# A second-half row of inverse deviations through DRAM instead of TensorE, in a fused conformer convolution layer

## The chip, the cores and the metric

One Trainium2 chip, one core. The metric is the device time of the kernel in microseconds (us); the kernel before took 353.53 us, the median of three runs (353.43 to 353.73). The engines go by short names: PE is TensorE, DVE is VectorE, ACT is ScalarE, POOL is GpSimd, SP is SyncE, which issues most DMAs. Each engine works through its own list in order; semaphores order the engines against each other.

## The reference

With one layer, the reference is an RMS norm, a gated depthwise convolution with a layer norm, and an output projection, added to x. Tokens T = 1024, channels D = 1024, 31 taps, all in float32:

```
hn = x * rsqrt(mean(x*x)) * norm_g
a, b, gate = split(hn @ w_in, 3)
u = causal_conv(a * sigmoid(b), conv_w) + conv_b         # per channel
uf = (u - mean(u)) * rsqrt(var(u) + eps) * ln_g + ln_b   # over channels
y = x + (silu(uf) * silu(gate)) @ w_out
```

## The kernel before

Activations lie with channels on the partitions: 8 channel tiles (k) of 128, and two halves (h) of 512 tokens. To keep float32 precision every matmul operand is split into a high part (x_hi, w_hi, wb_hi; made by ACT) and a remainder (x_lo, w_lo, wb_lo; made by DVE or POOL), and each product is three matmuls of 128 x 512.

The input projection is 24 units of 128 output channels (m = 0 to 23: pairs b and a, then 8 gates), each for both halves, 8 steps of three matmuls (`project`). The convolution runs behind it on DVE, ACT and POOL. The layer norm needs sums over channels, so over partitions: ACT and DVE split the convolution's words in two planes, a DMA transposes them, ACT and DVE join them (`join_half`, L932 and L1207), DVE takes statistics with tokens on the partitions (`take_stats`, `moments`), and POOL makes the inverse deviations (`inverse_deviation`, L1427), 128 x 4 numbers for each half. To use them with channels on the partitions again, a row of 512 tokens has to stand on all 128 partitions. For that PE multiplies a broadcast column by the identity (`spread_mean`, `spread_rstd`), four columns for each half and each of the two quantities, put between the steps of units 22 and 23 (`MEAN_SPREAD_AT`, `RSTD_SPREAD_AT`: unit, half, step). The result is in PSUM (`norm_spread`); ACT copies the deviations to SBUF as well (`copy_rstd`), because POOL's share of the first half's scalings (`POOL_SCALES`) reads them there.

Then, tile by tile: DVE subtracts the mean (`centre`), DVE or POOL multiplies by the deviation (`scale`), ACT applies SiLU with ln_g and ln_b into one of two PSUM banks (`act_norm`, which waits for the bank that the gate two tiles earlier frees), DVE multiplies by the gate (`gate`), and ACT and DVE split the result (`split_v`).

The output projection is done as seven block products (b = 0 to 6, `out_product`) of sums of blocks, a Strassen-like scheme; each has 4 pieces q of 128 tokens with 12 matmuls each. PE waits at a block's start for its operands (`wait_operands`: the x_lo by DVE, the wb_lo by DVE or POOL), and at each piece for a free bank, which an addition on DVE (`post`) frees. The sums of operands are `sum_v` on DVE and `w_out_op` on POOL, where `W_PAUSES` lets POOL wait for DVE's splits. All orders are written out by hand: the lists at the top, and each engine's own program in its block.

The lines that the rows name: L654 units' matmuls, L711 and L721 the spreads of means and deviations, L730 output products; L1211 DVE's half of the join, L936 ACT's; L1199 statistics, L1217 moments, L1223 `centre`, L1244 and L1470 `scale` on DVE and POOL, L1252 `gate`, L1259 `split_v`, L1279 `sum_v`, L1291 `post`; L947 `act_norm`, L851 reads a unit, L961 ACT's `split_v`; L1434 deviations, L1478 weight remainders of the output, L1462 those of the input; L930 the split of words; L671 and L798 the first units and x splits; L1158 the convolution's input.

Of the kernel before, what the change touches and what calls it, by code (L numbers as in the profile page):

```python
# [5 lines left out]
F32 = mybir.dt.float32  # L6
# [5 lines left out]
P = 128  # L12
# [28 lines left out]
MEAN_SPREAD_AT = {(22, 1, 2): 0, (22, 1, 6): 1}  # L41
RSTD_SPREAD_AT = {(22, 1, 4): 0, (23, 0, 0): 1}
# [32 lines left out]
SPREAD_AT = {1: (0, 4), 0: (3, 0, 1)}  # L75
CK = 4
# [23 lines left out]
def gated_conv_layer(nc, x, x_t, w_first, w_in, w_out, per_channel, identity, out):  # L100
# [31 lines left out]
    with ctx:  # L132
# [52 lines left out]

        acc = ctx.enter_context(nc.psum_tensor("acc", [P, 4, HALF], F32))
# [54 lines left out]
        rstd_ready = sem("rstd_ready")  # L241
        mean_spread = sem("mean_spread")
# [63 lines left out]
        def norm_spread(h, what):  # L306

            return acc[:, 2 * h + what, :]

# [201 lines left out]
        def _(sp):  # L511
# [79 lines left out]
            sp.wait_ge(wlo_ready, NU - 3)  # L591
            load_w_out("a", 0, 0, 1)
            sp.wait_ge(steps_done, len(STEPS))
            sp.wait_ge(sums_done, len(SUMS))
            load_w_out("b", 1, 0, 0)
            load_w_out("a", 1, 0, 1)
            for i in range(2):
                sp.wait_ge(wb_done, W_OP["lo", 0, i])
                load_w_out("b", i, 1, 0)
# [186 lines left out]
        def _(act):  # L786
# [151 lines left out]
            def copy_rstd(h):  # L938

                act.wait_ge(rstd_spread, h + 1)  # L940
                nc.scalar.activation(rstd_row(h), norm_spread(h, 1), ACT.Copy).then_inc(rstd_copied, 1)
# [67 lines left out]
            for m in range(2, NU):  # L1009
# [6 lines left out]
                for i, h in enumerate(half_order(m)):  # L1016
# [13 lines left out]
                    if (m, h) == (NU - 2, 1):  # L1030
                        copy_rstd(0)
                        for k in range(2):
                            act_norm(k, 0)
                    if (m, h) == (NU - 1, 0):
                        for k in range(2, 4):
                            act_norm(k, 0)
                        copy_rstd(1)
                        for k in range(4, 6):
                            act_norm(k, 0)
                    if (m, h) == (NU - 1, 1):  # L1040
                        for k in range(CK):
                            split_v(0, k)
                        act_norm(6, 0)
                        act_norm(7, 0)
# [36 lines left out]
        def _(dve):  # L1081
# [287 lines left out]
            for k in range(CK):  # L1369
                scale(k, 1)  # L1370
            for k in range(CK, KC):
                centre(k, 1)
            for k in range(CK):
                split_v(0, k)
# [8 lines left out]
            for k in range(2, KC):  # L1383
                gate(k, 1)
            posts(1, (0,))
            for k in range(CK):
                sum_v(2, k)
            posts(1, (1,))
            for k in range(CK):
                split_v(2, k)  # L1390
# [25 lines left out]
            posts(4, (2,))  # L1416
# [4 lines left out]
            posts(4, (3,))  # L1421
# [4 lines left out]
        def _(pool):  # L1426
# [27 lines left out]
            def finish_w_lo(m):  # L1454

                pool.wait_ge(whi_ready, m - 1)
                if m == 2:
                    nc.gpsimd.tensor_tensor(w_lo[:, 2, 0:KC // 2, :].rearrange("p k n -> p (k n)"), raw[:, 0, 0:HALF],
                                            w_hi[:, 2, 0:KC // 2, :].rearrange("p k n -> p (k n)").bitcast(F32),
                                            ALU.subtract).then_inc(w2lo_half_ready, 1)  # L1460
                ks = slice(KC // 2 if m == 2 else 0, KC)
                nc.gpsimd.tensor_tensor(w_lo[:, m % 3, ks, :].rearrange("p k n -> p (k n)"), raw[:, m % 2, ks.start * P:],  # L1462
                                        w_hi[:, m % 3, ks, :].rearrange("p k n -> p (k n)").bitcast(F32),
                                        ALU.subtract).then_inc(wlo_ready, 1)
# [86 lines left out]
            for h in range(NH):  # L1551
                inverse_deviation(h)
                w_out_op(*W_OPS[h])
# [56 lines left out]
```

## Time and profile before

| | |
|---|---|
| median of 3 runs | 353.53 us (353.43 to 353.73) |
| the profiled execution | 355.37 us, span from first to last instruction 353.6 us |
| PE busy | 348.6 us, 99%, 1564 matmuls |
| DVE busy | 323.1 us, 91% |
| ACT busy | 229.7 us, 65% |
| POOL busy | 258.9 us, 73% |
| granted TensorE clock | 1.0 of full speed in all 40 slices |
| chain that ended last | PE 92%, DMA 3%, SP's queue 3%, ACT 1% |

The busy shares say which engine has no idle time. The chain of waits is followed back from the last instruction, at each step to what released it, and so tells whose time the end depends on. The timelines give single instructions: start, duration, engine, line, what is written from what, and in brackets the idle time before it and what ended that.

### The profile page before, as it was taken

The page shows a single profiled execution, that of the slowest core. Times are in us where ns is not written, and L with a number is a line of the kernel's source. Part 1 is how long each engine was busy: PE and PEld are TensorE (multiplying, and loading weights), DVE is VectorE, ACT ScalarE, POOL GpSimd, SP SyncE. Part 2 cuts the span into 40 slices and gives each one's busy share as a digit, 9 for nine tenths or more (in the row PEclk, how much of TensorE's full clock was granted, in tenths as well). Part 3 has the DMA queues.
Part 4 walks back from the last instruction along what each step waited for, and adds up shares of the span by engine and source line. Part 5 has one row for each costly group of instructions (what it writes and reads, how often), then busy time and mean ns, then how long its engine had stood idle before and what let it go on. Part 6 is the DMA issues. An engine that isn't in the chain of part 4 may idle for free.

```text
span 353.6 us, 4764 instructions
## 1 busy us (share of the span) xinstructions
PE 348.6 (99%) x1564; PEld 289.3 (82%) x1564; DVE 323.1 (91%) x523; ACT 229.7 (65%) x330; POOL 258.9 (73%) x189
## 2 busy tenths in 40 slices
PE   8989999999999999999999999999999999999996
PEld 7868888888888888888888888888888888888886
DVE  4759799999999999999999999999699999999962
ACT  5979784667947780998669777984576773443400
POOL 0027999999999999689999999897596550406150
PEclk9999999999999999999999999999999999999999
DMA  7995111111410141404110410441743399074142
GB/s 253 411 412 196 61 61 53 66 62 59 119 48 14 62 119 59 119 0 121 59 44 19 119 59 3 119 119 38 235 145 119 93 371 346 25 239 142 68 177 90
DMA packets 30520, 43.51 MB, mean 123 GB/s; under 512 B 18336, under 2 KB 18848, under 8 KB 30496
## 3 DMA queue, kind: packets, MB, share of 16 engines
q1 hardware_dynamic: 30352, 43.21, 36.5%
q8 instruction: 12, 0.20, 0.2%
q14 instruction: 12, 0.10, 0.1%
q10 hardware_dynamic: 144, 0.00, 0.0%
HBM read 34.82 MB, written 4.19 MB: 110 GB/s over the span
## 4 chain that ended last, share of the span: by engine, by line
PE 92%; DMA 3%; SPq 3%; ACT 1%; issue 0%; DVE 0%
PE mm L654 68%; PE acc L730 12%; PE mm L730 9%; DMA sgate<-x 3%; SPq L518 2%; PE mm L671 2%; SPq L542 1%; PE acc L711 1%; PE acc L721 1%; SPq L514 0%; ACT sgate L792 0%; PE acc L648 0%; ACT x_hi L798 0%; PE acc L642 0%; SPq L548 0%
## 5 line engine op out<-in xcount | busy, mean ns | idle before, releaser
L654 PE MATMUL mm<-x_hi,w_hi 128*128 128x512 f32 x352 | 137.4, 390 | 0.0
L654 PE MATMUL mm<-x_hi,w_lo 128*128 128x512 f32 x352 | 137.0, 389 | 0.0
L654 PE MATMUL mm<-x_lo,w_hi 128*128 128x512 f32 x352 | 137.0, 389 | 0.0
L1191 DVE SCALAR_TENSOR_TENSOR acc<-u,chan,acc 128x512 f32<-128x512 f32 x157 | 110.8, 751 | 0.1
L1518 POOL TENSOR_TENSOR pconv<-pconv,prod 128x512 f32<-128x512 f32 x60 | 77.0, 1304 | 1.3 <-ACT prod L885 1.3
L654 PEld LDWEIGHTS mm<-x_hi,w_lo 128*128 128x128 f32 x352 | 66.1, 188 | 13.8
L654 PEld LDWEIGHTS mm<-x_hi,w_hi 128*128 128x128 f32 x352 | 66.1, 188 | 13.6
L654 PEld LDWEIGHTS mm<-x_lo,w_hi 128*128 128x128 f32 x352 | 66.1, 188 | 13.4
L1191 DVE SCALAR_TENSOR_TENSOR acc<-u,w_sum,acc 128x512 f32<-128x512 f32 x90 | 67.6, 752 | 2.1 <-ACT acc L867 2.0
L885 ACT ACTIVATE prod<-u,chan 128x512 f32<-128x512 f32 x69 | 47.9, 715 | 19.4 <-POOL pconv L1518 18.1
L1462 POOL TENSOR_TENSOR w_lo<-raw,w_hi 128x1024 fp32r<-128x1024 f32 (+1 forms) x21 | 49.6, 2362 | 7.6 <-ACT w_hi L834 7.6
L1518 POOL TENSOR_TENSOR pool_before<-pool_before,prod 128x512 f32<-128x512 f32 x37 | 48.1, 1301 | 1.1
L885 ACT ACTIVATE prod<-u,w_sum 128x512 f32<-128x512 f32 x30 | 21.4, 715 | 7.7 <-POOL pool_before L1518 7.4
L961 ACT ACTIVATE x_hi<-sgate 128x512 fp32r<-128x512 f32 x28 | 15.9, 624 | 15.7 <-DVE sgate L1279 15.7
L730 PE MATMUL acc<-wb_hi,x_hi 128*128 128x512 f32 (+1 forms) x68 | 25.7, 378 | 0.0
L730 PE MATMUL acc<-wb_hi,x_lo 128*128 128x512 f32 (+1 forms) x68 | 25.6, 377 | 0.0
L730 PE MATMUL acc<-wb_lo,x_hi 128*128 128x512 f32 (+1 forms) x68 | 25.6, 377 | 0.0
L834 ACT ACTIVATE w_hi<-raw 128x1024 fp32r<-128x1024 f32 x22 | 23.1, 1048 | 1.7 <-PE mm L654 1.7
L1478 POOL TENSOR_TENSOR wb_lo<-raw,wb_hi 128x1024 fp32r<-128x1024 f32 x5 | 12.0, 2399 | 14.3 <-DVE x_lo L1259 14.3
L911 ACT ACTIVATE sgate<-nat 128x1024 uint16<-128x1024 uint16 x14 | 14.0, 1049 | 11.5 <-POOL nat L1509 8.9
L924 ACT ACTIVATE rows<-sgate 128x1024 uint16<-128x1024 uint16 x14 | 18.3, 1372 | 3.6 <-DMA sgate<-sgate 2.3
L1451 POOL TENSOR_TENSOR x_lo<-nat,x_hi 128x512 fp32r<-128x512 f32 x16 | 20.2, 1304 | 0.0
(114 smaller groups left out, 520.8 us busy)
## 6 DMA issues: line engine op xcount, KB each, us to landing
raw<-w_in SPq DMA_DIRECT2D x22, 512.0 KB, 3.3
nat<-x_t SPq DMA_DIRECT2D x16, 256.0 KB, 6.0
sgate<-x SPq DMA_DIRECT2D x8, 512.0 KB, 11.6
raw<-w_out SPq DMA_DIRECT2D x8, 512.0 KB, 3.3
nat<-x SPq DMA_DIRECT2D x8, 512.0 KB, 7.7
y<-nat SPq DMA_DIRECT2D x15, 256.0 KB, 2.1
raw_late<-w_out SPq DMA_DIRECT2D x4, 512.0 KB, 4.2
sig<-w_out SPq DMA_DIRECT2D x4, 512.0 KB, 4.5
```

Source lines behind the costliest of these rows:

```text
L654: ins = nc.tensor.matmul(bank(("unit", m, h)), w[:, m % 3, k, :], xx[:, k, half(h)], start=(k == 0 and i == 0), stop=(k == KC - 1 and i == 2))
L730: ins = nc.tensor.matmul(product_bank(b, q), v[:, k0 + k, rows], w[:, k, piece_columns(b, q)], start=(k == 0 and i == 0 and continued(b, q ...
L834: nc.scalar.activation(w_hi[:, m % 3, :, :].rearrange("p k n -> p (k n)"), raw[:, m % 2, :], ACT.Copy).then_inc(whi_ready, 1)
L885: nc.scalar.activation(dst, chain_in(j, chain, k), ACT.Identity, scale=tap(j, chain, k), bias=bias(j, chain) if k == 0 else 0.0).then_inc( ...
L911: nc.scalar.activation(planes()[:, i * T:(i + 1) * T].rearrange("p (h s q) -> p h s q", h=NH, s=2), words(nat[:, j, :])[:, :, i].rearrange ...
L924: nc.scalar.activation(words_of_rows(side)[:, :, :, i], crossed()[:, NT * i:NT * (i + 1), :], ACT.Copy).then_inc(rows_joined, 1)
L961: nc.scalar.activation(v_pair(b, k)[0], v_raw(b, k), ACT.Copy).then_inc(vhi_ready, 1)
L1191: ins = nc.vector.scalar_tensor_tensor(dst, chain_in(j, chain, k), tap(j, chain, k), chain_bank(j, chain), ALU.mult, ALU.add)
L1451: nc.gpsimd.tensor_tensor(x_lo[:, k, half(h)], nat[:, k, half(h)], x_hi[:, k, half(h)].bitcast(F32), ALU.subtract).then_inc(xlo_pool, 1)
L1462: nc.gpsimd.tensor_tensor(w_lo[:, m % 3, ks, :].rearrange("p k n -> p (k n)"), raw[:, m % 2, ks.start * P:], w_hi[:, m % 3, ks, :].rearran ...
L1478: ins = nc.gpsimd.tensor_tensor(lo, source, hi.bitcast(F32), ALU.subtract)
L1518: ins = nc.gpsimd.tensor_tensor(pool_sum(chain), summand, prod[:, SLOTTED.index((j, chain, k)) % 4, :], ALU.add)
```

## The change

 - The second half's deviations are no longer spread by PE. SP stores the 128 x 4 numbers to a DRAM tensor and loads them back to all partitions as one row of 512 in the order token, tile; ACT copies the row to the PSUM bank that the spread used to fill, with the two orders swapped (a read with a step of four elements). This copy stands behind the activations of tiles 4 and 5, where the copy before stood ahead of them.
 - POOL makes both halves' deviations ahead of the first output weights' remainders; it did one, a remainder, the other, a remainder.
 - POOL's last remainder of the input weights waits for DVE's first copy of the join. SP loads one output weight ahead of that remainder's end.
 - PE spreads the means two steps sooner, the first half's deviations one step sooner, and the first half's root means (`SPREAD_AT`, at the start of the kernel) one step later.
 - On DVE, block 0's splits go ahead of four centrings, the first two additions of block 1 go ahead of two gates and two `sum_v`, and block 4's third additions go behind the operands of block 6.

```diff
--- before.py
+++ after.py
@@ -38,8 +38,8 @@
 ROWS_AT = {(7, 0): 0, (10, 0): 2, (12, 0): 1, (13, 1): 3, (16, 1): 5, (18, 1): 6, (20, 0): 4}
 CROSS_AFTER = {10: 0, 13: 2, 15: 1, 16: 3, 19: 5, 21: 6, 23: 4}
 STATS_AT = {10: [0], 14: [1], 19: [2]}
-MEAN_SPREAD_AT = {(22, 1, 2): 0, (22, 1, 6): 1}
-RSTD_SPREAD_AT = {(22, 1, 4): 0, (23, 0, 0): 1}
+MEAN_SPREAD_AT = {(22, 1, 0): 0, (22, 1, 4): 1}
+RSTD_SPREAD_AT = {(22, 1, 3): 0}
 POOL_SCALES = {0: (1, 3, 5, 7), 1: ()}
 
 
@@ -72,7 +72,7 @@
 ROW_ORDER = (4, 5, 6, 7, 0, 1, 2, 3)
 ROWS_BEFORE = {1: (4,), 2: (5,), 3: (6,), 4: (7,)}
 DIAGS_BEFORE = {4: (4, 5), 5: (6, 7)}
-SPREAD_AT = {1: (0, 4), 0: (3, 0, 1)}
+SPREAD_AT = {1: (0, 4), 0: (3, 0, 2)}
 CK = 4
 V_SOURCE = ((0, 0), (4, 0), (0, 0), (4, 1), (4, 1), (0, 1), (4, 0))
 V_SLOT = ((0, 0), (4, 0), (0, 1), (4, 1), (0, 0), (4, 0), (0, 1))
@@ -182,6 +182,8 @@
                 spare = sb("spare", [P, 2, KC * P])
             wb[slot] = [sb(f"wb_{part}{slot}", [P, CK, HALF], F32R) for part in ("hi", "lo")]
         raw_late = sb("raw_late", [P, KC * P])
+
+        rstd_dram = nc.dram_tensor("rstd_of_tokens", [P * TPH], F32, kind="Internal").ap()
 
         acc = ctx.enter_context(nc.psum_tensor("acc", [P, 4, HALF], F32))
         mm = ctx.enter_context(nc.psum_tensor("mm", [P, 4, HALF], F32))
@@ -239,6 +241,8 @@
         mv_ready = sem("mv_ready")
         veps_ready = sem("veps_ready")
         rstd_ready = sem("rstd_ready")
+        rstd_stored = sem("rstd_stored")
+        rstd_row_in = sem("rstd_row_in")
         mean_spread = sem("mean_spread")
         rstd_spread = sem("rstd_spread")
         rstd_copied = sem("rstd_copied")
@@ -306,6 +310,14 @@
         def norm_spread(h, what):
 
             return acc[:, 2 * h + what, :]
+
+        def by_token(row):
+
+            return row.rearrange("p (q t) -> p t q", t=TPH)
+
+        def by_tile(row):
+
+            return row.rearrange("p (t q) -> p t q", t=TPH)
 
         def rstd_row(h):
 
@@ -588,12 +600,16 @@
             load_w_out("b", 0, 0, 0)
             for h in range(NH):
                 cross_half(h)
-            sp.wait_ge(wlo_ready, NU - 3)
-            load_w_out("a", 0, 0, 1)
             sp.wait_ge(steps_done, len(STEPS))
             sp.wait_ge(sums_done, len(SUMS))
             load_w_out("b", 1, 0, 0)
+            sp.wait_ge(wlo_ready, NU - 3)
+            load_w_out("a", 0, 0, 1)
             load_w_out("a", 1, 0, 1)
+            sp.wait_ge(rstd_ready, NH)
+            sp.dma_start(rstd_dram.rearrange("(p t) -> p t", t=TPH), rstd[:, TPH:NT]).then_inc(rstd_stored, 16)
+            sp.wait_ge(rstd_stored, 16)
+            sp.dma_start(rstd_row(1), rstd_dram.partition_broadcast(P)).then_inc(rstd_row_in, 16)
             for i in range(2):
                 sp.wait_ge(wb_done, W_OP["lo", 0, i])
                 load_w_out("b", i, 1, 0)
@@ -935,10 +951,15 @@
                 act.wait_ge(stats_ready, NT * (KC // 2 - 1))
                 nc.scalar.activation(half_rows(h, 0), half_crossed(h, 0), ACT.Copy).then_inc(rows_joined, 1)
 
-            def copy_rstd(h):
-
-                act.wait_ge(rstd_spread, h + 1)
-                nc.scalar.activation(rstd_row(h), norm_spread(h, 1), ACT.Copy).then_inc(rstd_copied, 1)
+            def copy_rstd_row():
+
+                act.wait_ge(rstd_row_in, 16)
+                nc.scalar.activation(by_tile(norm_spread(1, 1)), by_token(rstd_row(1)), ACT.Copy).then_inc(rstd_copied, 1)
+
+            def copy_rstd():
+
+                act.wait_ge(rstd_spread, 1)
+                nc.scalar.activation(rstd_row(0), norm_spread(0, 1), ACT.Copy).then_inc(rstd_copied, 1)
 
             def act_norm(k, h):
 
@@ -1028,15 +1049,15 @@
                         act.wait_ge(sums_done, len(SUMS))
                         split_w_out(0, 0)
                     if (m, h) == (NU - 2, 1):
-                        copy_rstd(0)
+                        copy_rstd()
                         for k in range(2):
                             act_norm(k, 0)
                     if (m, h) == (NU - 1, 0):
                         for k in range(2, 4):
                             act_norm(k, 0)
-                        copy_rstd(1)
                         for k in range(4, 6):
                             act_norm(k, 0)
+                        copy_rstd_row()
                     if (m, h) == (NU - 1, 1):
                         for k in range(CK):
                             split_v(0, k)
@@ -1368,10 +1389,10 @@
             gate(3, 0)
             for k in range(CK):
                 scale(k, 1)
+            for k in range(CK):
+                split_v(0, k)
             for k in range(CK, KC):
                 centre(k, 1)
-            for k in range(CK):
-                split_v(0, k)
             for k in range(CK):
                 gate(CK + k, 0)
             for k in range(CK, KC):
@@ -1380,12 +1401,16 @@
             gate(1, 1)
             for k in range(CK):
                 split_v(1, k)
-            for k in range(2, KC):
+            for k in range(2, 6):
                 gate(k, 1)
             posts(1, (0,))
-            for k in range(CK):
+            for k in range(6, KC):
+                gate(k, 1)
+            for k in range(2):
                 sum_v(2, k)
             posts(1, (1,))
+            for k in range(2, CK):
+                sum_v(2, k)
             for k in range(CK):
                 split_v(2, k)
             for i in range(2):
@@ -1413,12 +1438,11 @@
                 split_v(5, k)
             posts(4, (1,))
             finish_wb_lo(5, 1)
-            posts(4, (2,))
             for k in range(CK):
                 sum_v(6, k)
             for k in range(CK):
                 split_v(6, k)
-            posts(4, (3,))
+            posts(4, (2, 3))
             for b in range(5, 7):
                 posts(b)
 
@@ -1454,6 +1478,8 @@
             def finish_w_lo(m):
 
                 pool.wait_ge(whi_ready, m - 1)
+                if m == NU - 1:
+                    pool.wait_ge(rows_by_vector, 1)
                 if m == 2:
                     nc.gpsimd.tensor_tensor(w_lo[:, 2, 0:KC // 2, :].rearrange("p k n -> p (k n)"), raw[:, 0, 0:HALF],
                                             w_hi[:, 2, 0:KC // 2, :].rearrange("p k n -> p (k n)").bitcast(F32),
@@ -1550,7 +1576,8 @@
             assert (due, summed) == (NU, KC)
             for h in range(NH):
                 inverse_deviation(h)
-                w_out_op(*W_OPS[h])
+            for op in W_OPS[0:2]:
+                w_out_op(*op)
             for k in POOL_SCALES[0]:
                 scale(k, 0)
             w_out_op(*W_OPS[2])
```

## Rows read from the trace of the kernel before

**Rows 1.** The page's busy engines: us, share of the span, instructions.
```profile
PE 348.6 (99%) x1564; PEld 289.3 (82%) x1564; DVE 323.1 (91%) x523; ACT 229.7 (65%) x330; POOL 258.9 (73%) x189
```

**Rows 2.** PE's waits: who waited for whom, us in total, times, longest.
```profile
PE mm L671 <- ACT x_hi L798: 1.1, 1, 1.1
```

**Rows 3.** The chain that ended last, in order: start, us, what.
```profile
255.74 0.89 PE acc L711 x8
...
262.58 0.89 PE acc L721 x8
```

**Rows 4.** Timeline of PE, output products: start, us, engine, line, operation.
```profile
274.20 0.47 PE L730 MATMUL acc<-wb_hi,x_hi 128*128 128x512 f32 x1
...
301.53 0.39 PE L730 MATMUL acc<-wb_hi,x_hi 128*128 128x512 f32 x1
...
328.73 0.39 PE L730 MATMUL mm<-wb_hi,x_hi 128*128 128x512 f32 x1
...
340.97 0.39 PE L730 MATMUL mm<-wb_hi,x_hi 128*128 128x512 f32 x1
```

**Rows 5.** Timeline of DVE, from the join to block 0's splits.
```profile
250.28 1.49 DVE L1211 COPY rows<-sgate 128x512 uint16<-128x512 uint16 x1 [2.64 <-DMA sgate<-sgate]
251.81 1.41 DVE L1199 BATCH_NORM_STATS2 stats<-rows 128x6 f32<-128x256 f32 x4
...
253.79 0.40 DVE L1211 COPY rows<-sgate 128x512 uint16<-128x512 uint16 x1
...
255.67 0.63 DVE L1217 BATCH_NORM_AGGREGATE mean_var<-stats 128x2 f32<-128x24 f32 x4
...
263.85 1.28 DVE L1252 TENSOR_TENSOR sgate<-mm,sgate 128x512 f32<-128x512 f32 x2
...
267.44 1.28 DVE L1252 TENSOR_TENSOR sgate<-mm,sgate 128x512 f32<-128x512 f32 x2
268.63 2.47 DVE L1244 TENSOR_TENSOR nat<-nat,acc 128x512 f32<-128x512 f32 x4
...
273.41 2.49 DVE L1259 TENSOR_TENSOR x_lo<-sgate,x_hi 128x512 fp32r<-128x512 f32 x4
```

**Rows 6.** Timeline of ACT: its half of the join, two activations.
```profile
250.28 0.79 ACT L936 ACTIVATE rows<-sgate 128x512 uint16<-128x512 uint16 x1 [0.82 <-DMA sgate<-sgate]
...
268.22 1.49 ACT L947 ACTIVATE mm<-nat,chan 128x512 f32<-128x512 f32 x2 [1.58 <-DVE sgate L1252]
```

**Rows 7.** Timeline of POOL: second deviations, scalings.
```profile
258.06 1.02 POOL L1434 TENSOR_TENSOR rstd<-var_eps,half_neg 128x4 f32<-128x4 f32 x1
...
261.40 5.06 POOL L1470 TENSOR_TENSOR nat<-nat,rows 128x512 f32<-128x512 f32 x4
```

**Rows 8.** Timelines of DVE and of POOL, from block 1 on.
```profile
287.92 1.40 DVE L1252 TENSOR_TENSOR sgate<-mm,sgate 128x512 f32<-128x512 f32 x2 [0.21 <-ACT mm L947]
...
289.83 2.49 DVE L1279 TENSOR_TENSOR sgate<-sgate 128x512 f32<-128x512 f32 x4
...
299.91 0.69 DVE L1291 TENSOR_TENSOR nat<-acc,nat 128x512 f32<-128x512 f32 x1
...
287.24 2.42 POOL L1478 TENSOR_TENSOR wb_lo<-sig,wb_hi 128x1024 fp32r<-128x1024 f32 x1
...
325.79 2.40 POOL L1478 TENSOR_TENSOR wb_lo<-raw,wb_hi 128x1024 fp32r<-128x1024 f32 x1 [2.43 <-DVE x_lo L1259]
...
338.32 2.43 POOL L1478 TENSOR_TENSOR wb_lo<-sig,wb_hi 128x1024 fp32r<-128x1024 f32 x1
```

**Rows 9.** ACT copies: group (busy, mean ns, idle) and line (ns min/median/max).
```profile
L961 ACT ACTIVATE x_hi<-sgate 128x512 fp32r<-128x512 f32 x28 | 15.9, 624 | 15.7 <-DVE sgate L1279 15.7
...
L930 ACT ACTIVATE sgate<-nat x2: 613/624/635, 246.9 to 247.4; 128x512 uint16<-128x512 uint16 x2
```

**Rows 10.** A small DMA: count, KB each, median us from issue to landing.
```profile
chan<-per_channel ACTq DMA_DIRECT2D x1, 4.0 KB, 2.4
```

**Rows 11.** Timeline of DVE at 118 us.
```profile
118.42 0.69 DVE L1158 TENSOR_TENSOR u<-mm,sig 128x512 f32<-128x512 f32 x1 [0.79 <-PE mm L654]
```

## The prediction

> **What bounds the kernel now.** I read the page's busy shares first: TensorE (PE) is at work 99% of the span [rows 1]. Then the list of PE's waits: once it is warmed up, its one wait is 1.1 us for the first split of x, near 23 us [rows 2]. From there to the end PE never stands still, and the chain of waits is one PE instruction after another. So the time falls by what leaves PE, as long as nothing that PE needs comes later than PE does. The spreads stand in this chain: four columns of means, and later four columns of inverse deviations, each half costing PE 0.89 us [rows 3].
>
> Next I compared when PE takes an operand with when it was made. The first output product (block 0) starts at 274.20 [rows 4]; DVE's first x_lo for it, the first of four of 0.69 us at a pitch of 0.60, ended at 273.41 + 0.69 = 274.10 [rows 5]. So 0.10 us after DVE is enough, and there is no room left. Block 6's second weight remainder ended on POOL at 338.32 + 2.43 = 340.75 [rows 8]; PE took it at 340.97 on its usual pitch [rows 4], so 0.22 us after POOL is enough, and there is none left here either. For block 5 POOL ended at 325.79 + 2.40 = 328.19 [rows 8] and PE came at 328.73 [rows 4]: 0.54, less 0.22, leaves 0.32 us. In block 2 the third bank is free when DVE's addition ends at 299.91 + 0.69 = 300.60 [rows 8]; PE came at 301.53 [rows 4]: 0.93, less 0.10, leaves 0.83. These margins decide: PE is the bound, with DVE and POOL right behind it.
>
> **The change part by part.**
>
> *Four matmul columns leave PE.* The second half's spread of deviations goes: -0.89 us [rows 3], if PE can use it.
>
> *Sooner join.* DVE's first copy of the join took 1.49 us where the same copy takes 0.40 with POOL idle; POOL's last remainder of the input weights ran beside it. POOL now waits for that copy, which ends at 250.28 + 0.40 = 250.68. ScalarE's half of the join ends at 250.28 + 0.79 = 251.07 [rows 6] and now decides: the statistics start at 251.1, not 251.81 [rows 5], 0.7 us sooner. All of the second half's moments, which ended at 255.67 + 0.63 = 256.30 [rows 5], end at 255.6. What queues behind POOL's new wait is that 2.40 us remainder, then ending near 253.2; PE wants it only in the last unit, past 262.58 [rows 3]. The means' spread moves six matmuls ahead, by 1.4 us, from 255.74 [rows 3] to about 254.3; the first moments end near 253.2, so PE doesn't wait.
>
> *Deviations ahead of the first output weights.* POOL's second deviation ended at 258.06 + 1.02 = 259.08 [rows 7] and would now end 1.3 us behind the moments, near 257.0. Behind it POOL does both remainders (2.40 each, as the one at 325.79 [rows 8]), which end at 261.8; before, its scalings began at 261.40 [rows 7]. So POOL's scalings start 0.4 later, although all ahead of them became sooner. SP's load behind the first remainder goes out at 259.4; nothing awaits it before POOL's subtractions, which stand behind the splits at 273 [rows 5].
>
> *Through DRAM.* Two DMAs one behind the other on SP, the second waiting for the first to land. The trace has no such store or broadcast; the nearest small transfer is 4 KB in 2.4 us [rows 10]. From 257.0, two of these land at 261.8. The row is not asked for before 269 (below), so each could take 6 us. Behind SP's wait stands only the load just named. I count 0; the other end is a row that lands late (a rival). SP also sends one output weight load ahead of its wait for POOL and another behind it; ScalarE's splits of these stand ahead of its copy of the first half's row, for which DVE comes at 255.6 + 8 x 0.60 = 260.4. I count 0, hidden by these eight centrings; up to 0.4 late would still reach nothing, because gate 1 waits for POOL anyway (below); past that it costs DVE its full lateness.
>
> *The row's copy on ScalarE.* This is what I think costs the most. It used to stand ahead of the activations of channel tiles 4 and 5, and DVE's scalings of the second half could start at 268.63 right behind the gates [rows 5]. Now it stands behind them. These two activations wait for the banks that DVE's gates 2 and 3 free: they began at 268.22, 0.10 us after the first of these gates ended, and took 1.49 together [rows 6].
>  - Where the gates come: POOL's first scaling starts at 261.8 and takes 1.30 (four in a row took 5.06 [rows 7]), the activation that needs it some 0.75 (a half of 1.49 [rows 6]), so gate 1 starts at 263.85 where it was 263.85 + 0.60 = 264.45 [rows 5]. Gates 2 and 3 come 0.6 sooner too: gate 2 runs from 266.84 to 267.52, not from 267.44 [rows 5].
>  - Then 267.52 + 0.10 = 267.62, plus 1.49 for the two activations is 269.11, plus the copy.
>  - The copy: 512 elements of SBUF, read with a step of four elements, into a bank. Not in the trace. A plain SBUF copy of that size takes 0.62, and one that reads every second 16-bit word 0.61 to 0.64 [rows 9]; one that writes with such a step took 0.79 [rows 6]. I take 0.62, the nearest row, and keep 0.61 to 0.79 and, as a rival, twice 0.62.
>  - So DVE's four scalings start at 269.7, not 268.63: 1.1 us later, with DVE idle for 1.5 us ahead of them.
>
> The Trainium skill, page "SBUF — State Buffer", section "Specifications (TRN2)", says that a 16-byte line of SBUF wants two hits or more for full bandwidth and that each new line costs something. The 16-bit row above has several elements in a line and shows no loss; no run here reads one element in 16 bytes, which is what this copy does. By the row the sum below stands; by the rule the copy is dearer, and the last rival holds.
>
> *Splits ahead of the centrings.* The x_lo of block 0 now follow the four scalings: 269.7 + 2.39 + 0.69 = 272.8. PE comes at 274.20 - 0.89 = 273.31, so it passes with 0.4 to spare. Without this swap PE would have waited. Everything else in that stretch is the same twelve DVE instructions, so the gates of tiles 4 to 7 and what hangs on them in turn (ScalarE's last activations, block 1's splits) come 1.1 us late.
>
> *Additions.* The first addition of block 1 now goes between the second half's gates 5 and 6, where DVE waited 0.2 us twice for ScalarE (one of the two: [rows 8]). That gives back 0.4 us, of which POOL's remainder takes 0.14: it ends at 287.24 + 2.42 = 289.66, and the first subtraction, at 289.83 before and 289.42 now (both plus 1.1), waits for its end less a lead of about 0.1 [rows 8]. DVE goes on 1.1 - 0.27 = 0.8 us late. The second addition, two subtractions sooner, is 1.2 us sooner by that, which covers its own bank. The addition that moves behind block 6's splits puts these three additions sooner (1.8 us), so block 6's remainder no longer binds.
>
> *The first half's root-mean spread one step later.* Three matmuls, about 0.68 us (half of the 1.4 above): DVE gets its scale that much later, and DVE waits for PE by 0.79 at 118.42 [rows 11], which swallows it. Zero; without that wait it would add up to 0.68 to DVE's lateness.
>
> **The sum.** DVE is 0.8 late from 290 us on. In block 2, 0.8 against a margin of 0.83: PE is back at its old time, the 0.89 is gone. POOL's remainder for block 5 hangs on DVE's last split before it, and DVE shows no idle time between: 0.8 late against a margin of 0.32, PE is 0.8 - 0.32 = 0.48 us later than before. Behind that nothing is tighter, and the tail follows PE. The profiled execution took 355.37 us, 1.8 over its span of 353.6; by the sum it becomes 355.85. The median of the runs, 353.53, lies at the span; the same 0.48 makes it 354.0.
>
> **Rivals.**
>  - *The saving comes through: 352.65* (353.53 - 0.89). For: PE alone bounds today, and three of the reorderings hit just the places with the least margin. Against: DVE would have to be 0.57 us sooner at block 5 (0.89 - 0.32), and I find it 0.8 late.
>  - *No lateness: 353.2.* If POOL doesn't hold up gate 1 (0.4) and the waits on ScalarE give back twice what I count (0.4), DVE comes to block 5 as before, and 0.89 - (0.89 - 0.32) leaves a gain of 0.32. For: I add many small terms. Against: DVE's order and the two activations ahead of the copy are fixed by semaphores.
>  - *The strided copy is slow: 354.6.* One mechanism: the copy takes 1.24, DVE's scalings start 0.62 later still, and 0.48 + 0.62 = 1.1. It turns the verdict to slower from a copy of about 0.85 us on (0.48 + 0.23 = 0.71).
>  - *The row arrives late.* The change then doesn't do what it says: if the two DMAs take over 12 us, ScalarE waits for DRAM; each microsecond past 269 costs one. At 1 us, 355.0. Against: 2.4 us each.
>
> **How the numbers follow.** The forecast gets 0.52, within 353.6 to 354.4 by itself; the full saving 0.19; no lateness 0.12; the slow copy 0.14; the late row 0.03 (1.00 in all). A difference of 0.2%, 0.7 us, is what measurements of this kernel can tell. Faster: the full saving, 0.19. Slower: slow copy, late row and 0.05 of the forecast's own tail, 0.22. Same: the rest of the forecast and the case without lateness, 0.59. The range reaches from the full saving to the slow copy, 352.6 to 354.7, and leaves out the late row and the tails.
>
> **What would show it.** Right: no PE time at the second half's deviations; DVE's join copy at 0.40; an idle DVE of some 1.5 us ahead of the scalings near 269.7, ended by ScalarE's copy; PE waits of some tenths at the third bank of block 2 and at the start of block 5, the latter for POOL. Wrong: scalings that start by 268.6, or a PE without waits, with 0.89 us off the span; a copy of over 0.9 us or one that waits for its DMA.

## The result and the profile after

The changed kernel takes 355.04 us (median of 12 runs, 354.67 to 356.41); the kernel before took 353.75 in the same comparison (12 runs, 353.19 to 354.80). The ratio is 1.0039 [1.0029, 1.0050]: 1.3 us slower, where 354.0 was forecast from 353.53, 0.5 slower. The profiled execution took 354.73 us, span 352.9.

Two spans can't be set against each other as they stand. In the profile of before PE had waited 1.1 us for x near 23 us [rows 2]; the changed kernel's profile has no such wait, and neither have two later profiles of the kernel before, whose spans are 351.8 and 351.6. So I count from the first matmul of the units. Here it is in the kernel before, with the last unit matmul and the last product on PE:

```profile
30.23 0.39 PE L654 MATMUL mm<-x_hi,w_hi 128*128 128x512 f32 x1
...
273.98 0.39 PE L654 MATMUL mm<-x_hi,w_lo 128*128 128x512 f32 x1
...
350.52 0.28 PE L730 MATMUL acc<-wb_hi,x_lo 128*128 128x256 f32 x1
```

The same view of the changed kernel, and between these rows every place where PE stood still after the units:

```profile
28.25 0.39 PE L670 MATMUL mm<-x_hi,w_hi 128*128 128x512 f32 x1
...
255.21 1.05 PE L737 MATMUL acc<-ident,rstd 128*128 128x128 f32 x8
...
271.10 0.39 PE L670 MATMUL mm<-x_hi,w_lo 128*128 128x512 f32 x1
271.76 0.47 PE L746 MATMUL acc<-wb_hi,x_hi 128*128 128x512 f32 x1 [0.28 <-issue]
...
282.51 0.39 PE L746 MATMUL mm<-wb_hi,x_lo 128*128 128x512 f32 x1
283.05 0.47 PE L746 MATMUL acc<-wb_hi,x_hi 128*128 128x512 f32 x1 [0.15 <-issue]
...
291.10 0.39 PE L746 MATMUL acc<-wb_hi,x_lo 128*128 128x512 f32 x1
291.41 0.50 PE L746 MATMUL acc<-wb_hi,x_hi 128*128 128x512 f32 x1
...
299.50 0.39 PE L746 MATMUL mm<-wb_hi,x_lo 128*128 128x512 f32 x1
300.30 0.50 PE L746 MATMUL acc<-wb_hi,x_hi 128*128 128x512 f32 x1 [0.42 <-DVE nat L1312]
...
327.44 0.39 PE L746 MATMUL mm<-wb_hi,x_lo 128*128 128x512 f32 x1
327.99 0.47 PE L746 MATMUL mm<-wb_hi,x_hi 128*128 128x512 f32 x1 [0.17 <-POOL wb_lo L1504]
...
349.87 0.28 PE L746 MATMUL acc<-wb_hi,x_lo 128*128 128x256 f32 x1
```

Only one spread of deviations is left (at 255.21). The last unit matmul comes 271.10 - 28.25 = 242.85 us after the first; before it was 273.98 - 30.23 = 243.75. The 0.9 us really left PE. But the last product comes at 349.87 - 28.25 = 321.62 against 350.52 - 30.23 = 320.29, 1.33 later. In between PE lost 2.2 us. Its pitch is 0.227; the gaps at the starts of block 0, 1 and 5 exceed it by 0.43, 0.31 and 0.32, those inside block 1 and block 2 by 0.08 and 0.57, together 1.7, and the matmul behind each pause follows 0.08 to 0.11 later than its pitch too, together 0.5. PE's list of waits, which had one entry after the warm-up [rows 2], names them:

```profile
PE acc L746 <- issue: 0.4, 2, 0.3
PE acc L746 <- DVE nat L1312: 0.4, 1, 0.4
PE mm L746 <- POOL wb_lo L1504: 0.2, 1, 0.2
```

The list leaves out part of each pause (0.28 of 0.43 at block 0), so the gaps between rows are the better measure. The busy shares hardly moved, against [rows 1]: PE still 99%.

```profile
PE 348.1 (99%) x1556; PEld 288.5 (82%) x1556; DVE 322.1 (91%) x523; ACT 230.4 (65%) x330; POOL 259.1 (73%) x189
```

Why the operands are late is read from DVE's timeline, the answer to [rows 5]:

```profile
244.49 0.69 DVE L1202 TENSOR_TENSOR nat<-nat,acc 128x511 f32<-128x511 f32 x1
...
248.62 0.46 DVE L1232 COPY rows<-sgate 128x512 uint16<-128x512 uint16 x1 [2.64 <-DMA sgate<-sgate]
249.50 1.41 DVE L1220 BATCH_NORM_STATS2 stats<-rows 128x6 f32<-128x256 f32 x4 [0.42 <-ACT rows L952]
...
262.28 0.69 DVE L1273 TENSOR_TENSOR sgate<-mm,sgate 128x512 f32<-128x512 f32 x1 [0.51 <-ACT mm L968]
...
265.28 1.28 DVE L1273 TENSOR_TENSOR sgate<-mm,sgate 128x512 f32<-128x512 f32 x2
268.58 2.48 DVE L1265 TENSOR_TENSOR nat<-nat,acc 128x512 f32<-128x512 f32 x4 [2.02 <-ACT acc L957]
270.98 2.49 DVE L1280 TENSOR_TENSOR x_lo<-sgate,x_hi 128x512 fp32r<-128x512 f32 x4
```

The join's copy takes 0.46 in place of 1.49. Then, behind gates 2 and 3 (265.28), DVE stands idle for 2.02 us: ScalarE's copy of the row (L957) ends that. The scalings start 268.58 - 28.25 = 240.33 after the first unit matmul, before 268.63 - 30.23 = 238.40: 1.93 late. On ScalarE, the answer to [rows 6], the two activations stand ahead of the copy, and the copy takes 1.06:

```profile
266.06 1.49 ACT L968 ACTIVATE mm<-nat,chan 128x512 f32<-128x512 f32 x2 [1.92 <-DVE sgate L1273]
267.49 1.06 ACT L957 ACTIVATE acc<-rows 128x512 f32<-128x512 f32 x1
```

The row itself was there long before. SP's issues, and the time from issue to landing of the two transfers (us, last column of the list of DMA issues):

```profile
255.48 0.33 SPq L610 DMA_DIRECT2D rstd_of_tokens<-rstd  x1
257.49 0.33 SPq L612 DMA_DIRECT2D rows<-rstd_of_tokens  x1
```
```profile
rows<-rstd_of_tokens SPq DMA_DIRECT2D x1, 256.0 KB, 4.1
...
rstd_of_tokens<-rstd SPq DMA_DIRECT2D x1, 2.0 KB, 2.0
```

257.49 + 4.1 = 261.6, and the copy began at 267.49. Last, POOL, for [rows 7, 8]: its second deviations, its scalings, and the remainder that block 5 waits for.

```profile
254.43 1.02 POOL L1458 TENSOR_TENSOR rstd<-var_eps,half_neg 128x4 f32<-128x4 f32 x1
...
260.13 5.07 POOL L1496 TENSOR_TENSOR nat<-nat,rows 128x512 f32<-128x512 f32 x4
...
325.44 2.41 POOL L1504 TENSOR_TENSOR wb_lo<-raw,wb_hi 128x1024 fp32r<-128x1024 f32 x1 [2.43 <-DVE x_lo L1280]
```

This remainder ends 327.85 - 28.25 = 299.60 after the first unit matmul; before, 328.19 - 30.23 = 297.96. It is 1.64 late, and that less the margin of 0.32 that the prediction found there is 1.32, PE's loss.

### The profile page after: what moved, and what is told of

It reads as the page before. It is cut to its first block, busy times and chain, and to the rows that moved or that the text cites. A ratio compares the mean times of both kernels' runs of the same rounds, so it can differ in the third digit from the quotient of the medians.

```text
span 352.9 us, 4751 instructions
## 1 busy us (share of the span) xinstructions
PE 348.1 (99%) x1556; PEld 288.5 (82%) x1556; DVE 322.1 (91%) x523; ACT 230.4 (65%) x330; POOL 259.1 (73%) x189
## 4 chain that ended last, share of the span: by engine, by line
DVE 38%; POOL 21%; issue 19%; ACT 8%; PE 6%; DMA 4%; SPq 3%; DVEq 0%; ACTq 0%; POOLq 0%
DVE acc L1212 20%; POOL x_lo L1475 5%; POOL pconv L1544 5%; POOL w_lo L1488 4%; PE mm L746 3%; PE acc L746 3%; DMA raw<-w_in 3%; DVE x_lo L1280 3%; DVE nat L1244 2%; DVE stats L1220 2%; POOL pool_before L1544 2%; SPq L530 2%; DVE sgate L1300 2%; POOL u L1522 2%; DVE nat L1312 2%
## 5 line engine op out<-in xcount | busy, mean ns | idle before, releaser
L1544 POOL TENSOR_TENSOR pconv<-pconv,prod 128x512 f32<-128x512 f32 x60 | 79.4, 1379 | 1.3 <-ACT prod L901 1.3
L1488 POOL TENSOR_TENSOR w_lo<-raw,w_hi 128x1024 fp32r<-128x1024 f32 (+1 forms) x21 | 50.8, 2419 | 9.6 <-DVE rows L1232 5.6
L1544 POOL TENSOR_TENSOR pool_before<-pool_before,prod 128x512 f32<-128x512 f32 x37 | 50.2, 1356 | 1.1
```

Of the source, the lines that this page charges most:

```text
L1544: ins = nc.gpsimd.tensor_tensor(pool_sum(chain), summand, prod[:, SLOTTED.index((j, chain, k)) % 4, :], ALU.add)
```

## The experiments

The theory: the copy's new place, behind two activations, makes DVE late, and PE gives back more than the spread cost. Rivals: the copy's stepped read (its length, not its place); the path through DRAM; the shifted root-mean spread; and that the margins read from the profile of before were wrong. Times are medians (of one run each in the last experiment), ratios are to the kernel before in the same comparison (353.59 and 353.63 us).

**Read and write without a step.** The store goes to DRAM in the order tile, token, so that ScalarE reads the row straight.

```diff
-sp.dma_start(rstd_dram.rearrange("(p t) -> p t", t=TPH), rstd[:, TPH:NT]).then_inc(rstd_stored, 16)
+sp.dma_start(rstd_dram.rearrange("(t p) -> p t", t=TPH), rstd[:, TPH:NT], allow_slow_non_contiguous=True).then_inc(rstd_stored, 16)
...
-nc.scalar.activation(by_tile(norm_spread(1, 1)), by_token(rstd_row(1)), ACT.Copy).then_inc(rstd_copied, 1)
+nc.scalar.activation(norm_spread(1, 1), rstd_row(1), ACT.Copy).then_inc(rstd_copied, 1)
```

> The store writes the 512 numbers to DRAM tile by tile (512 pieces of 4 bytes), so that ScalarE's copy reads the row without a step; its place is unchanged. Theory A (the copy's place behind two activations and its step make DVE's second-half scalings late, and the lateness reaches PE): the copy takes 0.6 us and not 1.06, DVE's idle time ahead of the scalings goes from 2.0 to about 1.6, and the time falls by about 0.45 us, to 354.6. Theory B (the lateness comes from the DMAs through DRAM or from the earlier edits, not from this copy): no change, 355.0. Theory C (the row lands too late): the slower store makes it worse, over 355.0.

Measured: 356.86 us, ratio 1.0087 [1.0073, 1.0101]. The edit cured one thing and broke another. Its ScalarE row and its store:

```profile
270.43 0.60 ACT L957 ACTIVATE acc<-rows 128x512 f32<-128x512 f32 x1 [2.56 <-DMA rows<-rstd_of_tokens]
```
```profile
rstd_of_tokens<-rstd SPq DMA_DIRECT2D x1, 2.0 KB, 9.7
```

The straight copy takes 0.60, so the step costs 0.46. But the store is now 512 pieces of 4 bytes and needs 9.7 us instead of 2.0, and ScalarE waits 2.56 us for the row: the prediction's late row, made by hand. As a test of the copy's length it is spoiled; the sixth experiment repeats it.

**The copy first.** The row's copy goes ahead of the activations of tiles 4 and 5.

```diff
+                        copy_rstd_row()
                         for k in range(4, 6):
                             act_norm(k, 0)
-                        copy_rstd_row()
```

> Only the copy of the row moves: ahead of the activations of tiles 4 and 5, where the copy before stood; step and DRAM path stay. Theory A: the scalings follow the gates with no idle time, 2.0 us sooner than in the changed kernel, PE's waits in the output products all but go (some 0.1 us left at block 5), and most of the 0.89 us is kept: about 0.75 us under the kernel before, 353.0. Theory B: the time stays at 355.0, or falls by at most a few tenths. Theory C: the copy waits for its DMA, holds up the two activations, and the time is not better than 355.0.

Measured: 354.01 us, ratio 1.0012 [1.0003, 1.0021]. 1 us better than the change, not the 2 expected. Rows of ScalarE, of POOL, and DVE's first three block-0 splits as one group (ns min/median/max):

```profile
264.48 1.08 ACT L957 ACTIVATE acc<-rows 128x512 f32<-128x512 f32 x1
```
```profile
267.93 2.42 POOL L1504 TENSOR_TENSOR wb_lo<-sig,wb_hi 128x1024 fp32r<-128x1024 f32 x1
```
```profile
L1280 DVE TENSOR_TENSOR x_lo<-sgate,x_hi x3: 677/679/1640, 269.3 to 271.4; 128x512 fp32r<-128x512 f32 x3
```

The copy finds its row (no wait in its line), and DVE's idle time of 2.02 is gone. But the sooner splits now begin at 269.3, while POOL's remainder runs until 267.93 + 2.42 = 270.35, and the first of them takes 1.64 us instead of 0.68: a microsecond lost to a neighbour that the late version had missed by accident.

**The root-mean spread back where it was.**

```diff
-SPREAD_AT = {1: (0, 4), 0: (3, 0, 2)}
+SPREAD_AT = {1: (0, 4), 0: (3, 0, 1)}
```

> Only the first half's root-mean spread goes back to one step sooner. Theory A: DVE catches up with PE near 118 us either way, so no change within 0.15 us of the changed kernel, 355.0. Theory B (part of DVE's lateness is made at the start): 0.3 us or more under the changed kernel, 354.7 or less.

Measured: 355.21 us, ratio 1.0047 [1.0035, 1.0060], which overlaps that of the changed kernel. Two rows of DVE:

```profile
116.86 0.69 DVE L1179 TENSOR_TENSOR u<-mm,sig 128x512 f32<-128x512 f32 x1 [0.75 <-PE mm L670]
...
249.73 0.47 DVE L1232 COPY rows<-sgate 128x512 uint16<-128x512 uint16 x1 [3.25 <-DMA sgate<-sgate]
```

DVE's wait for PE near 117 us is back at 0.75, as in [rows 11]; in the changed kernel it was 0.17. Behind it DVE starts 88.19 us after the first unit matmul in all three kernels, so that wait did swallow DVE's share of the shift. POOL's share comes below. The second row is chance: here the transposes landed 0.6 us later than in the changed kernel's profile (3.25 of waiting against 2.64), so the rest of this profile says nothing on the shift.

**The place alone.** The kernel before, with only its copy of the deviations moved behind the two activations.

```diff
-                        copy_rstd(1)
                         for k in range(4, 6):
                             act_norm(k, 0)
+                        copy_rstd(1)
```

> The kernel before, with one edit: its copy of the second half's spread (from a bank, 0.58 us) moves behind the activations of tiles 4 and 5. Theory A: DVE's scalings start 1.6 us later (0.10 + 1.49 + 0.58 behind gate 2 in place of 0.51), block 0's splits, which stand behind them and have no margin, hand all of it to PE: 1.6 us slower than the kernel before, 355.3. Theory B: the place of the copy costs nothing that PE feels, 353.7.

Measured: 355.40 us, ratio 1.0047 [1.0035, 1.0060]. One line moved is enough for a slowdown of this size, without DRAM, without a stepped read (0.58 here), without a new order on DVE or POOL. ScalarE's copy, and PE's one wait after the warm-up:

```profile
268.21 0.58 ACT L941 ACTIVATE rows<-acc 128x512 f32<-128x512 f32 x1
```
```profile
PE acc L730 <- DVE nat L1223: 1.5, 1, 1.5
```

PE loses 1.5 us at block 0 in one piece, because here the centrings still stand ahead of its splits.

**Copy first, and POOL paused.** The second experiment, and POOL's remainder of the last of the first four output weights waits until block 0's splits are done.

```diff
 w_out_op(*W_OPS[2])
+pool.wait_ge(vlo_ready, CK)
 w_out_op(*W_OPS[3])
```

> The copy of the row first (as in the run before this one with that edit), and POOL's second remainder of block 1's weights waits for block 0's four splits on DVE. Theory A1 (what was left, 0.4 us over the kernel before, is DVE's first split held up for 0.95 us by that remainder): the split takes 0.69 us again and not 1.64, DVE is 0.95 us sooner from there on, PE waits only at block 5, 0.1 to 0.2 us, and the time is 0.75 us under the kernel before, 352.85. Rival A2 (it is the DRAM path or the order of the additions that costs it): 0.4 us over the kernel before, 354.0, as without the pause.

Measured: 353.01 us, ratio 0.9983 [0.9973, 0.9993], faster than both kernels. Block 0's splits run at their old pace, and PE's waits hold nothing but the warm-up:

```profile
269.64 2.50 DVE L1280 TENSOR_TENSOR x_lo<-sgate,x_hi 128x512 fp32r<-128x512 f32 x4
```
```profile
PE acc L792 <- DVE ones L1103: 1.0, 1, 1.0
```

So 1.0 us (354.01 to 353.01) was the price of that collision.

**The row read straight, from the same transfers.** The changed kernel, where ScalarE's copy reads the row without the step, and so leaves out putting the deviations in the order of the tokens.

```diff
-nc.scalar.activation(by_tile(norm_spread(1, 1)), by_token(rstd_row(1)), ACT.Copy).then_inc(rstd_copied, 1)
+nc.scalar.activation(norm_spread(1, 1), rstd_row(1), ACT.Copy).then_inc(rstd_copied, 1)
```

> The changed kernel, with ScalarE's copy reading the row straight through and not with a step of four: the second half's deviations then stand against the wrong tokens; store, load and the copy's place are unchanged. Theory A: the copy takes 0.62 us and not 1.06, all behind it is 0.44 us sooner, 0.4 to 0.45 us off the changed kernel's time (354.6 to 354.75). Rival (a step costs nothing, or what it costs is hidden): as the changed kernel, 355.1.

Measured: 354.36 us, ratio 1.0024 [1.0015, 1.0033].

```profile
267.55 0.58 ACT L957 ACTIVATE acc<-rows 128x512 f32<-128x512 f32 x1
```

The copy is 0.48 shorter and the kernel 0.5 to 0.7 (by PE's last product 0.51). With a copy of the length that I had assumed, the change would still be 0.7 to 0.8 us slower than before.

**Copy first and POOL paused, but with PE's spread.** The DRAM path is taken out again; PE spreads the second half's deviations and the copy reads the bank.

```diff
-RSTD_SPREAD_AT = {(22, 1, 3): 0}
+RSTD_SPREAD_AT = {(22, 1, 3): 0, (23, 0, 0): 1}
...
-                act.wait_ge(rstd_row_in, 16)
-                nc.scalar.activation(by_tile(norm_spread(1, 1)), by_token(rstd_row(1)), ACT.Copy).then_inc(rstd_copied, 1)
+                act.wait_ge(rstd_spread, 2)
+                nc.scalar.activation(rstd_row(1), norm_spread(1, 1), ACT.Copy).then_inc(rstd_copied, 1)
```

> As the run with the pause, but without the DRAM path: PE spreads the second half's deviations as it did before, and the copy reads the bank. All other edits stay. Theory A: PE has its 0.89 us back and no waits, so the kernel takes what the kernel before takes, 353.6 within 0.2, and 0.75 us more than with the pause and the DRAM path. Rival (the DRAM path costs as much as it saves, by its DMAs): the two are equal within 0.2 us.

Measured: 353.80 us, ratio 1.0006 [0.9997, 1.0015]. 353.80 - 353.01 = 0.79: the DRAM path gives back nearly all of the 0.89, once nobody waits for the row. With all the other edits in, the copy first and POOL paused, the kernel stands where it stood before (353.80 against 353.63). Only times are compared here.

**The kernel before once more, then three profiles together.** For the rival that the margins were wrong, and for an open point: in the first profile of before, DVE's last step of the convolution (L1181; L1202 in the changed kernel) began 246.15 - 30.23 = 215.92 after the first unit matmul, in the changed kernels 216.2 to 216.3.

```profile
246.15 0.69 DVE L1181 TENSOR_TENSOR nat<-nat,acc 128x511 f32<-128x511 f32 x1
```

> The kernel before, for a second profile: in the first, PE waited 1.1 us for a split of x at 22 us, and the execution took 1.8 us more than the median. Theory A: without that wait DVE stands 0.3 us later against PE from the last convolution step on (as it does in four profiles of changed kernels), so the margins of the prediction were 0.3 us too wide and PE waits about 0.3 us at block 0. Rival: the same distance as in the first profile, PE without waits; then the edits made DVE 0.3 us later.

Measured: 353.65 us, distance 215.87, PE's last product at 320.29 and block 5's remainder at 297.97, both as in the first profile. The margins stood.

> A third profile of the kernel before, for one open point: counted from the first matmul of the units on PE, DVE's last step of the convolution started 215.9 us later in both profiles of the kernel before and 216.2 to 216.3 in every changed one. Theory A (the phase in which POOL's work and PE's come out of the loads at the start scatters from run to run, whatever the kernel): 215.9 or 216.25 here, either may come, and over the three profiles sent together both values appear for one and the same program. Theory B (the program sets it): 215.9 again. Time 353.6 in both.

> The copy's place alone, profiled once more. Its code is that of the kernel before up to the place of the copy. Theory A: 215.9 or 216.25 for DVE's last step of the convolution. Theory B: 216.25 again; but its program is the same up to there, so B would have to rest on where the code lies. Time 355.3.

> The changed kernel, profiled once more. Theory A: 215.9 or 216.25; where it is 215.9, gate 1 comes 0.3 us sooner than in its first profile and the scalings with it. Theory B: 216.25 again. Time 355.0.

Measured, in this order: 353.39, 355.08 and 354.99 us; 216.37, 216.70 and 216.17. The kernel before's third profile, PE's first unit matmul and the step on DVE:

```profile
28.19 0.39 PE L654 MATMUL mm<-x_hi,w_hi 128*128 128x512 f32 x1
```
```profile
244.56 0.69 DVE L1181 TENSOR_TENSOR nat<-nat,acc 128x511 f32<-128x511 f32 x1
```

One program shows 215.9 twice and 216.37 once, the copy's place alone 216.25 and 216.70. So in one program this distance scatters from run to run by up to 0.5 us (theory A), and the profile on which I predicted lay at the early end. In the kernel before this hardly reaches the end: in its third profile gate 1 comes 234.24 after the first unit matmul, 234.22 in the other two, since DVE there waited 0.37 us for PE's spread of the means anyway. The wait in the first profile:

```profile
256.67 4.87 DVE L1223 TENSOR_TENSOR nat<-nat,acc 128x512 f32<-128x512 f32 x8 [0.37 <-PE acc L711]
```

The changed kernel spreads the means sooner, and its DVE shows no wait there.

But scatter is not all of it. The seven profiles of changed kernels lie closer together, from 216.17 to 216.33, and none shows 215.9. DVE's lateness comes in at one wait for ScalarE, at 154.93 in the first profile of before, 153.36 in its third, 153.26 in the changed kernel's first:

```profile
154.93 0.76 DVE L1191 SCALAR_TENSOR_TENSOR acc<-u,w_sum,acc 128x512 f32<-128x512 f32 x1 [0.86 <-ACT acc L867]
```
```profile
153.36 0.76 DVE L1191 SCALAR_TENSOR_TENSOR acc<-u,w_sum,acc 128x512 f32<-128x512 f32 x1 [1.31 <-ACT acc L867]
```
```profile
153.26 0.75 DVE L1212 SCALAR_TENSOR_TENSOR acc<-u,w_sum,acc 128x512 f32<-128x512 f32 x1 [1.17 <-ACT acc L883]
```

ScalarE goes by POOL there (in the kernel before it waits 19 times for POOL's part of the convolution, 18.4 us in all), and POOL keeps how late it is against PE: in the third profile of before 0.45 us at 14 us after the first unit matmul, and 0.46 still at 174. The moved root-mean spread makes POOL late. ScalarE's copy of that spread and POOL's next remainder of the input weights, in the first profile of before (two rows) and in the second of the changed kernel (two rows):

```profile
37.45 0.60 ACT L815 ACTIVATE pconv<-acc 128x512 f32<-128x512 f32 x1 [0.16 <-PE acc L648]
...
44.47 2.42 POOL L1462 TENSOR_TENSOR w_lo<-raw,w_hi 128x1024 fp32r<-128x1024 f32 x1
```
```profile
36.54 0.60 ACT L831 ACTIVATE pconv<-acc 128x512 f32<-128x512 f32 x1 [0.79 <-PE acc L664]
...
43.16 2.41 POOL L1488 TENSOR_TENSOR w_lo<-raw,w_hi 128x1024 fp32r<-128x1024 f32 x1 [0.15 <-ACT w_hi L850]
```

In that second profile the first unit matmul is at 28.64. ScalarE's copy starts 0.68 later against it (36.54 - 28.64 = 7.90 against 7.22), ScalarE's split of the weights, behind steps that need the spread, is late by the same 0.68 (13.40 against 12.72), and POOL waits for that and starts at 14.52 instead of 14.24. In all six profiles with the moved spread POOL starts this remainder at 14.52 to 14.60, though one step earlier it was only 0.06 to 0.36 behind the first profile of before. So with the edit POOL is never less than 0.28 behind that first profile; the edit itself adds what chance had not, 0 to 0.22 us in these six. In the profile of the spread put back, chance had made POOL 0.36 late already; that experiment could not show this, and its time, 355.21, is not below the changed kernel's either. What these tenths cost at the end, no run shows by itself.

What all these kernels have in common, counted from the first unit matmul: the lateness of block 5's remainder on POOL against 297.96, that less the 0.32 of the prediction, and the lateness of PE's last product against 320.29.

| kernel | remainder late | less 0.32 | PE late | time, us |
|---|---|---|---|---|
| the change | 1.64 | 1.32 | 1.33 | 355.04 |
| the change, once more | 1.52 | 1.20 | 1.25 | 354.99 |
| store in 512 pieces | 3.73 | 3.41 | 3.46 | 356.86 |
| copy first | 0.55 | 0.23 | 0.28 | 354.01 |
| spread back | 2.33 | 2.01 | 2.03 | 355.21 |
| row read straight | 1.13 | 0.81 | 0.82 | 354.36 |
| copy first, POOL paused | -0.47 | -0.79 | -0.74 | 353.01 |

In every row PE's lateness is DVE's and POOL's, less 0.32, to within 0.05. (The profiled execution of "spread back" was the slowest of its five runs, 355.85 us, with the late transposes shown above. Where only the place was moved, PE was 1.71 late already from block 0, and this rule did not decide.)

## Why the prediction was wrong, step by step

The mechanism was the forecast one, and so was its sign; the lateness that it makes was sized at 1.1 us and is 1.93. The step that failed is "The row's copy on ScalarE", by its two sizes: the copy (0.62, measured 1.06) and the gates ahead of it (0.6 us sooner, measured 0.19). Behind the second stands a term put at zero, the moved root-mean spread, besides a profile of before that lay at the early end of its scatter.

- *Four columns leave PE, -0.89:* right, 0.90 at the last unit matmul.
- *Sooner join:* the copy fell to 0.46 as said (0.40), but the statistics began 0.33 sooner (249.50 - 28.25 against 251.81 - 30.23), not 0.7. The work ahead of the join came 0.32 later than in the profile I read (216.24 against 215.92): scatter and, as shown above, the moved root-mean spread. The kernel before swallowed such a lateness at its wait for the means; the changed kernel passes it on.
- *POOL's scalings 0.4 later:* 0.71 (260.13 - 28.25 against 231.17), the same 0.3.
- *Gate 1 0.6 sooner:* 0.19 (262.28 - 28.25 = 234.03 against 234.22). 0.3 of the gap came with POOL; the chain from POOL's scaling over ScalarE to DVE took 2.15 instead of 2.05.
- *The copy, 0.62:* 1.06. I took the plain row [rows 9] and put the dearer copy into a rival at twice that; a copy of over 0.9 us was one of my own signs of being wrong. The straight reads of 0.58 and 0.60 beside stepped ones of 1.06 and 1.08 show that the step is the cause. The Trainium skill, page "SBUF — State Buffer", section "Specifications (TRN2)", asks for two hits or more in each 16-byte line; this copy makes one, and these rows agree with that. The other row that I leaned on, every second 16-bit word, has four words of each line read, so it could not speak for this read.
- *Scalings 1.1 late:* 1.93, which is 0.44 for the copy and 0.41 for gates 2 and 3 more than counted.
- *Block 0 passes with 0.4 to spare:* with 0.83 more lateness it can't, and PE lost 0.43 there; block 1 stumbled as well.
- *Additions give back 0.27:* 0.29 (1.93 at the scalings, 1.64 at block 5's remainder).
- *The DRAM row lands before it is asked for:* right, at 261.6 against 267.49, and the seventh experiment shows what the path gives back.
- *The root-mean spread later: zero.* Right for DVE, by the third experiment; wrong for POOL, which stays at least 0.28 behind the profile that I read.
- *Margin of 0.32 at block 5:* right to 0.05 in all seven rows of the table, by some luck. PE can begin 0.14 after POOL's end (327.99 against 327.85), not only after 0.22, so it waits only for what goes beyond 0.40; the matmul behind the pause then loses 0.08 more. With 1.64 in place of 0.8 the prediction's own sum gives 1.32; PE was 1.33 late, and the medians differ by 1.29.

Of the rivals, the slow copy was half of the miss; by itself, at the measured 1.06, it would have made 0.48 + 0.44 = 0.9. The full saving lost to the copy's place: with the copy ahead of the activations 0.6 to 0.8 of the 0.89 comes through, but only when POOL is held off the splits too. That the copy first would be enough was my next error. It met POOL's remainder, and a split of two SBUF operands began in earnest only near that remainder's end. The Trainium skill, page "SBUF — State Buffer", section "🔬 SBUF: two separate sides", says that a DVE operation with both inputs in SBUF and a GpSimd operation that reads SBUF exclude each other for whole instructions; 1.64 beside 0.68, and four splits in 2.50 once POOL was paused, agree with it.

## What to carry to other kernels

Where one engine is busy 99% of the time, measure how far each operand is ahead of it before taking work off it; here the margin was 0.32 us at one block, and all of DVE's lateness beyond it became time. When a step moves on an engine's list, price what now stands ahead of it and who waits for it: the place of one copy cost more than the matmuls that the change saved. Do so for every engine that waits for the step: the shift that DVE swallowed stayed with POOL. Read margins from more than one profile, for the head of the kernel shifts the engines against each other by some tenths, as much as the margins themselves.

## What the runs showed of the hardware that was not expected

- A ScalarE copy of 512 float32 from SBUF to PSUM takes 0.58 to 0.60 us read straight and 1.06 to 1.10 read with a step of four elements.
- A 2 KB store from SBUF to DRAM lands in 2.0 to 2.3 us as 128 pieces of 16 bytes, and in 9.7 us as 512 pieces of 4 bytes. The broadcast of that row to 128 partitions, 256 KB, takes 3.7 to 4.9.
- The same transposes by DMA let DVE wait 2.64 us in the first two profiles of the kernel before and 3.29 in the third.
- A DVE split with both operands in SBUF took 1.64 us where a remainder of POOL was running, and 0.68 alone.
